# HGRN2 layers: three four-block score visits of 192 columns in place of six two-block visits of 64, with masks kept for one tile

## The reference

```python
q, f, inp_v, g = split(rms_norm(x) @ w_in, 4)      # 1024 columns each
q = silu(q); k = (1 - lb) * sigmoid(-f); log_f = log(lb + (1 - lb) * sigmoid(f))
b = cumsum(log_f)                                   # within a chunk
decay = exp(where(causal, b[t] - b[s], NEG_BIG))
scores = einsum('tk,sk,tsk->ts', q, k, decay)       # decay differs by feature k
o = scores @ v + (q * exp(b)) @ state               # state carried from chunk to chunk
y = rms_norm(o) * o_norm_w * silu(g)
x = x + y @ w_out
```

## Time and profile before

| | before |
|---|---|
| median of 3 runs | 1531.73 us (1531.69 to 1532.85) |
| the profiled execution's own time | 1533.73 us |
| its span in the trace | 1531.9 us |
| TensorE matmul busy | 1455.2 us, 95% of the span |
| VectorE busy | 960.8 us, 63% |
| ScalarE busy | 666.2 us, 43% |
| mean granted TensorE clock | 0.986 of full speed |

### The profile page before, as it was taken

The page is one execution under the profiler, slowest core; times in us unless marked ns, Lnnn a source line. Parts: engine busy times, 40 slices in busy tenths (PEclk is TensorE's granted clock), DMA queues, the critical chain, the costliest instruction groups (busy, mean ns, idle before and its releaser), DMA issues.

```text
span 1531.9 us, 24253 instructions
## 1 busy us (share of the span) xinstructions
PE 1455.2 (95%) x9165; PEld 1301.1 (85%) x9165; DVE 960.8 (63%) x1755; ACT 666.2 (43%) x1174; POOL 6.5 (0%) x16
## 2 busy tenths in 40 slices
PE   7999999989999999999999996699998999999989
PEld 6888888789898989898989895599887988888878
DVE  6677777554566656565666564566656567676772
ACT  5333334233545454545555554344433333433340
POOL 1000000000000000000000000000000000000000
PEclk9999999999999999999999998899999999999999
DMA  6322222233131322222222220043333231322111
GB/s 191 83 61 78 55 66 71 59 100 110 43 97 51 89 56 83 62 78 69 70 70 69 70 70 28 11 120 102 89 99 105 57 83 56 83 56 81 55 55 56
DMA packets 211723, 114.30 MB, mean 75 GB/s; under 512 B 3742, under 2 KB 209744, under 8 KB 211632
## 3 DMA queue, kind: packets, MB, share of 16 engines
q1 hardware_dynamic: 211200, 112.54, 25.6%
q0 software_dynamic: 432, 0.47, 0.1%
HBM read 110.90 MB, written 2.10 MB: 74 GB/s over the span
## 4 chain that ended last, share of the span: by engine, by line
PE 74%; DVE 12%; ACT 8%; issue 5%; DMA 1%; SPq 0%; ACTq 0%; DVEq 0%
PE ps L530 34%; PE ps L542 22%; PE ps L664 5%; ACT scratch L1160 4%; PE ps L810 2%; PE ps L796 2%; PE ps L827 2%; DVE scratch L1682 2%; ACT w_hi L966 2%; DVE scratch L1706 2%; DVE scratch L1690 2%; DVE w_lo L1365 2%; PE ps L693 1%; PE ps L556 1%; PE ps L695 1%
## 5 line engine op out<-in xcount | busy, mean ns | idle before, releaser
L542 PE MATMUL ps<-w_hi,op_hi 128*128 128x256 f32 (+2 forms) x1280 | 418.1, 327 | 17.6 <-DVE op_lo L1409 7.1
L542 PE MATMUL ps<-w_lo,op_hi 128*128 128x256 f32 (+2 forms) x1280 | 404.1, 316 | 0.0
L542 PE MATMUL ps<-w_hi,op_lo 128*128 128x256 f32 (+2 forms) x1280 | 403.9, 316 | 0.0
L530 PE MATMUL ps<-op_hi,w_hi 128*128 128x512 f32 (+1 forms) x800 | 321.5, 402 | 2.2 <-DVE op_lo L1404 2.2
L530 PE MATMUL ps<-op_lo,w_hi 128*128 128x512 f32 (+1 forms) x800 | 307.1, 384 | 0.0
L530 PE MATMUL ps<-op_hi,w_lo 128*128 128x512 f32 (+1 forms) x800 | 306.0, 383 | 0.0
L1365 DVE TENSOR_TENSOR w_lo<-raw,w_hi 128x1024 fp32r<-128x1024 f32 x200 | 242.8, 1226 | 89.8 <-ACT w_hi L966 89.6
L542 PEld LDWEIGHTS ps<-w_hi,op_hi 128*128 128x128 f32 x1280 | 243.9, 191 | 37.3 <-issue 10.1
L542 PEld LDWEIGHTS ps<-w_lo,op_hi 128*128 128x128 f32 x1280 | 243.9, 191 | 5.6
L542 PEld LDWEIGHTS ps<-w_hi,op_lo 128*128 128x128 f32 x1280 | 244.4, 191 | 4.8 <-issue 0.2
L966 ACT ACTIVATE w_hi<-raw 128x1024 fp32r<-128x1024 f32 x200 | 205.1, 1057 | 45.8 <-PE ps L542 30.2
(11 more groups left out here) (174 smaller groups left out, 1571.3 us busy)
## 6 DMA issues: line engine op xcount, KB each, us to landing
raw<-in_b_w_in SPq DMA_DIRECT2D x80, 512.0 KB, 3.7
raw<-in_a_w_in SPq DMA_DIRECT2D x64, 512.0 KB, 4.3
raw<-in_c_w_in SPq DMA_DIRECT2D x24, 512.0 KB, 4.5
raw<-in_a_w_out SPq DMA_DIRECT2D x16, 512.0 KB, 4.3
raw<-in_b_w_out SPq DMA_DIRECT2D x8, 512.0 KB, 4.3
raw<-in_c_w_out SPq DMA_DIRECT2D x8, 512.0 KB, 4.6
xt<-in_x SPq DMA_DIRECT2D x4, 512.0 KB, 8.3
y<-in_norm_w SPq DMA_DIRECT2D x4, 512.0 KB, 4.7
```

Source lines behind the costliest of these rows:

```text
L530: last = nc.tensor.matmul(bank, a, b, start=(k == 0 and p == 0), stop=(k == KT - 1 and p == 2))
L542: last = nc.tensor.matmul(bank, a, b, start=(k == 0 and p == 0), stop=(k == KT - 1 and p == 2))
```

## The change

The six two-block visits with m = 2, 4, ..., 64 become three four-block visits (`quad_scores(r)`) with m = 2, 8, 32. A tile is cut into groups of four blocks of m tokens. The keys are multiplied with three of the four blocks of queries (blocks 1, 2, 3, as they are: 96 columns) and with the same three of a second array `a_far` (96 columns), in which queries have been carried one or two boundaries on: `far_queries` makes blocks 2 and 3, `farthest_queries` makes the one for three blocks back and puts it in the place of block 1. So a visit is four matmuls of 192 columns. Two PSUM banks become one array `scores2`, which each visit fills whole, so every visit waits until the copies of the one before it (`kept`) are done: for visit 0 these are the copies of `scores(0)` and `scores(1)`, `keep_own` and `keep_pairs`. VectorE makes three copies for each visit (384, 256 and 128 elements, `keep_quad(r, 1)` to `keep_quad(r, 3)`), and the masks are stored for one tile and read for all four. The moves stay seven of the queries and seven of the keys. `move_queries(0)` to `farthest_queries(0)` run at the head of the body, `turn_k`, `states` and `values` come one step later, and in body 8 the output splits and the columns of `wide` are placed anew. Cut to its core:

```diff
-G_STEPS = LEVELS + 1
+QUADS = (2, 8, 32)
+G_STEPS = 2 + len(QUADS)
+KEPT = 2 + 3 * len(QUADS)
+QUAD_MASK = 3 * P // 4 + P // 2 + P // 4
+MASKS = P + P // 2 + QUAD_MASK * len(QUADS)
...
                     def scores(g):
-                        q, k, bank = a_q[:, prev], a_k[:, prev], score[g % 2]
-                        if g < 2:
-                            pe.wait_ge(qk_lo_done, h + 1)
-                        else:
-                            pe.wait_ge(upd, h * LEVELS + (g - 1))
-                        if g >= 2:
-                            pe.wait_ge(sd_done, h * 8 + (g - 1))
-                        elif later and g == 0:
-                            pe.wait_ge(st_step, h * 3)
-                        elif later:
-                            pe.wait_ge(sd_done, h * 8)
...
-                            m = 1 << (g - 1)
-                            upper = q.rearrange("p (t b u m) -> p t b u m", t=TT, u=2, m=m)
-                            for t in range(TT):
-                                last = nc.tensor.matmul(bank[:, t * 64:(t + 1) * 64], k[:, t * P:(t + 1) * P],
-                                                        upper[:, t, :, 1, :], start=True, stop=True)
+                        bank = score[g]
+                        pe.wait_ge(qk_lo_done, h + 1)
+                        if later:
+                            if g == 0:
+                                pe.wait_ge(st_step, h * 3)
+                            pe.wait_ge(sd_done, h * KEPT)
+                        cols, to = (slice(0, S), bank[:]) if g == 0 else (slice(S, S + 256), bank[:, 0:256])
+                        nc.tensor.matmul(to, ones_sq, qk_hi[:, cols], start=True, stop=False)
+                        last = nc.tensor.matmul(to, ones_sq, qk_lo[:, cols], start=False, stop=True)
+                        last.then_inc(g_ready, 1)
+
+                    def quad_scores(r):
+
+                        m = QUADS[r]
+                        pe.wait_ge(far_done, h * 6 + 2 * r + 2)
+                        pe.wait_ge(sd_done, h * KEPT + 2 + 3 * r)
+                        for t in range(TT):
+                            tile = slice(t * P, (t + 1) * P)
+                            of = a_qq[:, prev, :, tile].rearrange("p x (h c) -> p x h c", c=4 * m)[:, :, :, m:]
+                            last = nc.tensor.matmul(scores2[:, t * 256:t * 256 + 192], a_k[:, prev, tile], of,
+                                                    start=True, stop=True)
                         last.then_inc(g_ready, 1)
 
...
                     if mix:
                         steps[1] = [turn_v]
-                        for g in range(G_STEPS):
-                            steps.setdefault(int(2 + 2.4 * g), []).append(lambda g=g: scores(g))
-                        steps[21] = [turn_k]
-                        steps[23] = [states]
-                        steps[27] = [values]
+                        for g, at in ((0, 2), (1, 4)):
+                            steps[at] = [lambda g=g: scores(g)]
+                        for r, at in ((0, 5), (1, 11), (2, 17)):
+                            steps[at] = [lambda r=r: quad_scores(r)]
+                        steps[22] = [turn_k]
+                        steps[24] = [states]
+                        steps[28] = [values]
...
                     if mix and not proj:
-                        for k, ks in enumerate((9, 11, 14, 16, 18, 21, 23)):
+                        for k, ks in enumerate((11, 11, 17, 17, 22, 22, 24)):
                             steps[ks].append(lambda k=k: wide(n, k, (0, 1)))
                         for k in range(KT - 3):
-                            steps[27].append(lambda k=k: wide(n, k, (2, 3)))
+                            steps[28].append(lambda k=k: wide(n, k, (2, 3)))
...
+                    def moved(n):
+                        dve.wait_ge(upd, h * LEVELS + n)
+
+                    def kept(count):
+                        dve.wait_ge(sd_done, h * KEPT + count)
+
+                    def far_queries(r):
+
+                        m = QUADS[r]
+                        nb = S // (4 * m)
+                        start = 2 * S - 2 * S // m
+                        decay = a_t[:, prev, start:start + 4 * nb].rearrange("p (b u) -> p b u", u=4)
+                        q = a_q[:, prev].rearrange("p (b u m) -> p b u m", u=4, m=m)
+                        far = a_far[:, prev].rearrange("p (b u m) -> p b u m", u=4, m=m)
+                        moved(2 * r + 1)
+                        nc.vector.tensor_tensor(far[:, :, 2:4], q[:, :, 2:4],
+                                                decay[:, :, 1:3].unsqueeze(3).to_broadcast([P, nb, 2, m]),
+                                                ALU.mult).then_inc(far_done, 1)
+
+                    def farthest_queries(r):
...
+                        dve.wait_ge(far_done, h * 6 + 2 * r + 1)
+                        nc.vector.tensor_tensor(far[:, :, 1], far[:, :, 3],
+                                                decay[:, :, 1].unsqueeze(2).to_broadcast([P, nb, m]),
+                                                ALU.mult).then_inc(far_done, 1)
+
+                    def keep_own():
+                        mask = a_mask[:, 0:P].unsqueeze(1).to_broadcast([P, TT, P])
+                        nc.vector.copy_predicated(a_sd, mask, score[0].rearrange("p (t c) -> p t c", t=TT)).then_inc(sd_done, 1)
+
+                    def keep_pairs():
+                        to = a_sd.rearrange("p t (b u) -> p t b u", u=2)[:, :, :, 1]
+                        mask = a_mask[:, P:P + 64].unsqueeze(1).to_broadcast([P, TT, 64])
+                        nc.vector.copy_predicated(to, mask, score[1][:, 0:256].rearrange("p (t b) -> p t b", t=TT)).then_inc(sd_done, 1)
+
+                    def keep_quad(r, back):
+
+                        m = QUADS[r]
+                        nb = P // (4 * m)
+                        to = a_sd.rearrange("p t (b c) -> p t b c", c=4 * m)[:, :, :, back * m:]
+                        of = scores2[:].rearrange("p (t c) -> p t c", c=256)[:, :, 0:192]
+                        of = of.rearrange("p t (x b c) -> p t x b c", x=2, b=nb)
+                        of = (of[:, :, 0], of[:, :, 1, :, m:], of[:, :, 1, :, 0:m])[back - 1]
+                        at = P + 64 + QUAD_MASK * r + (0, 96, 160)[back - 1]
+                        wide = 4 * m - back * m
+                        mask = a_mask[:, at:at + nb * wide].rearrange("p (b c) -> p b c", b=nb)
+                        nc.vector.copy_predicated(to, mask.unsqueeze(1).to_broadcast([P, TT, nb, wide]),
+                                                  of).then_inc(sd_done, 1)
...
-                    for g in range(8):
+                    if mix:
+                        move_queries(0)
+                        move_keys(0)
+                        far_queries(0)
+                        farthest_queries(0)
+                        if static(h) and h == 0:
+                            dve.wait_ge(s_mask, 16)
+                        if later:
+                            dve.wait_ge(o_ready, h)
+                        taken(0)
+                        gate()
+                        keep_own()
+                    if end:
+                        into_y()
+                    if mix:
+                        taken(1)
+                        kept(1)
+                    if proj:
+                        split_lo_chunk(IN0[n], len(A_PARTS), j, par, 2, a_ring)
+                    elif mix:
+                        split_lo_out(n, 2)
+                    if mix:
+                        keep_pairs()
+                    if proj:
+                        split_lo_chunk(IN0[n], len(A_PARTS), j, par, 3, a_ring)
+                    for r in range(len(QUADS)):
+                        last = r + 1 == len(QUADS)
                         if mix:
-                            taken(g)
-                            gate() if g == 0 else move_on(g)
-                            keep(g)
-                        if mix and not proj and g > 1:
-                            split_y(n, g - 2)
-                        if g == 0 and end:
-                            into_y()
-                        if mix and not proj and g in (1, 2):
-                            split_lo_out(n, g + 1)
-                        if mix and not proj and g in (5, 6, 7):
-                            split_lo_out(n, g - 1)
-                        if proj and g in (1, 2):
-                            split_lo_chunk(IN0[n], len(A_PARTS), j, par, g + 1, a_ring)
-                        if g == 3 and proj:
-                            forget()
-                        if g == 6 and proj:
-                            query()
-                        if g == 7 and proj:
-                            products()
-                        if g >= 4 and proj:
-                            decays({4: (0,), 5: (1, 2), 6: (3, 4), 7: (5, 6)}[g])
-                    if mix and not proj:
-                        split_y(n, 6)
```

(62 more changed lines are left out.)

53 lines of the change are left out of this document (22 added, 31 removed).

## The result

| | before | with the change |
|---|---|---|
| median of 4 runs each | 1532.28 us (1531.69 to 1532.85) | 1549.24 us (1547.27 to 1551.02) |
| the profiled execution's own time | 1533.73 us | 1551.02 us |
| its span | 1531.9 us | 1549.2 us |
| mean granted clock | 0.986 | 0.980 |

The ratio is 1.0108 (1.0092 to 1.0123): 1.1% slower. 1547 was forecast.

What follows compares the result with a forecast made beforehand. TensorE's own list was taken to bound the fourteen bodies with projection and mixing. Per head -1.35 + 1.64 + 0.5 = +0.8, 11.2 in fourteen, plus 4 for body 8: +15, so 1547 us, range 1534 to 1561.

Steps and rivals of the forecast that it cites:

- What the visits save: On TensorE, three visits of 1.31 us replace six of 0.88, saving 1.35 us a head.
- The first wait: TensorE before visit 0 waits for keep_pairs, behind chunk 2's low half on VectorE: 1.64 us a head.
- Visits 1 and 2: VectorE's chain between visits takes 3.7 us against 4.2 of steps, so TensorE has no wait, with 0.5 to spare.
- The second wait: TensorE before the values waits for the end of carry on VectorE: 0.5 us a head.
- The sum of a head: Saving and two waits together: -1.35 + 1.64 + 0.5 = +0.8 us a head, 11.2 in 14 heads.
- Body 8: VectorE's chain sets the time; TensorE waits some 7.5 us, gets back some 2: 2 us a layer, 4 in all.
- The layers between: No separate cost was forecast outside the heads and body 8; the rest was to cost nothing.
- The first wait only: Rival: the values find their states ready, so only the wait before visit 0 costs; 1540 us, chance 0.13.
- VectorE the bound: Rival: copies writing short runs cost the higher rate, so each visit waits, +1 us a head; 1561 us, chance 0.13.
- The visit bound by weight loads: Rival: 192-column records go at the 0.11 us of 64-column ones, a visit 0.9; 1529 us, chance 0.10 with similar ways.
- The falling clock: Rival: the wait in each head drops TensorE to 1.2 GHz, 3.4 us a head; 1595 us, chance 0.03.

Runs made afterwards that it cites:

- e8: e7 with scores(1) one step earlier, turn_o behind step 4 and keep_pairs ahead of into_y on VectorE; 1515.12 us, ratio 0.9886 to the kernel before.
- e1: The changed kernel with keep_pairs, and a memset of one column, ahead of the low half of chunk 2 on VectorE; 1530.40 us, ratio 0.9984.
- e2: The changed kernel with the three visits, turn_k, states and values each one step later; 1541.33 us, ratio 1.0053.
- e7: e4 with the low half of chunk 3 behind the copies of visit 1; 1523.38 us, ratio 0.9932 to the kernel before.
- e3: The changed kernel with only the values one step later, behind step 29; 1544.41 us, ratio 1.0071.
- e9: e8 with body 8 alone changed: output splits ahead of the visits, most wide steps earlier; 1509.84 us, ratio 0.9839 to the kernel before.
- e4: The changed kernel with the edits of e1 and e3 together; 1525.91 us, ratio 0.9952.
- e6: The changed kernel with visits of 96 columns instead of 192, the far queries not multiplied; 1528.16 us, ratio 0.9973.
- e5: The kernel before with masks stored for one tile and read for all four, nothing else; 1533.48 us, ratio 1.0000.

## Why the prediction was right

**What the visits save** was put at 1.35 us a head and is 1.56: 31.61 less 30.05, in e8, where no wait is left in a head. The cost of a new visit, 1.31, was right. The undisturbed step is 0.683 (four from 116.22 to 118.95); visit 1 takes 1.16 and 4.25 with the six steps behind it, so 1.16 + 4.25 - 4.10 = 1.31. The old visit was mis-sized: I took the step as 0.70 from the one behind `scores(1)`, which carries a surplus itself, and so found only 0.07 behind the visit. With 0.683 it is 0.81 + 2.15 - 2.05 = 0.91, and 6 x 0.91 - 3 x 1.31 = 1.53.

**The first wait** was put at 1.64 and is 1.60 + 0.11 = 1.71. The steps to it are there as written: the low half holds VectorE for 1.14, the copy takes 0.72, the signal 0.05, the first visit after a wait 0.11 more. e1 shows its cause and e2 that its length is what counts. e1 gives back only 0.90 of it: its copy still comes 0.25 of shown idle time late, and visit 1 is then late too, which e7 and e8 gave back with 0.30 and 0.52. With the 0.50 of e3 these are 2.22, and the two waits were 1.71 + 0.50 = 2.21.

**Visits 1 and 2** don't wait, as laid. The chain was put at 3.7 from the end of visit 0, signals included, and took 3.9 without the last signal (114.71 to 118.60), so it had 0.35 to spare instead of 0.5.

**The second wait** was put at 0.5; taking it away shortens a head by 0.50. The shown idle time is 3.5 us in fourteen heads, 0.25 each (0.53 at 134.94 is the longest); the overlap of 0.16 and the 0.10 by which the first group after it takes longer (0.71 against 0.61 in the earlier trace rows) make up the rest.

**The sum of a head** was +0.8 and is +0.66, by the larger saving; in fourteen heads 9.2 us instead of 11.2. **Body 8** was put at 4, 2 a layer. From the last q sigmoid of a layer to the square of its last `o_norm` (lines 1114 and 1126 on ScalarE) it takes 3.4 us more than before in layer 0 and 2.6 in layer 3, 6.0 together. TensorE waits there for 7.9 us of shown idle time in both layers, as laid (7.5); what was mis-sized is the 2 us that it should get back, which was 0.6 and 1.4. The clock accounts for the difference between the two layers at most. These are layer 3's visits 0 and 1 and the stretches at a low clock, first of layer 0, then of layer 3:

```profile
1485.35 2.90 PE L674 MATMUL scores<-scratch 128*128 128x192 f32 x8 [4.28 <-DVE scratch L1603]
1491.85 2.92 PE L674 MATMUL scores<-scratch 128*128 128x192 f32 x8 [3.60 <-DVE scratch L1592]
...
273.60:287.20 13.60, 9.27 (x25) 8.00 (x26) 9.55 (x23) 5.31 (x8) 0.00 (x0) 0.51 0.26 77
1483.60:1496.00 12.40, 7.05 (x21) 6.34 (x22) 8.50 (x17) 6.34 (x10) 0.00 (x0) 0.72 0.27 81
```

In layer 0 the clock stands at half for 13.6 us, twice as long as before; in layer 3, behind the same waits, it is at half for some 7 us in all, as before, and that body 8 is 2.6 us longer all the same.

**The layers between,** which the change doesn't touch, were put at nothing and were 1.8 us longer in the profiled execution: 943.3 us against 941.5, from the last `o_norm` of layer 0 to the first q sigmoid of layer 3, with 5943 records of TensorE in both. The clock stood at half for some 41 us of it, against 31 before (added up from stretches of 2 us). In the profiles of all eleven kernels the two go together: 939.9 to 941.5 us in the five with 31 us at half the clock, 941.0 in the one with 34, 941.8 to 943.3 in the five with 41. e8 lies in the first of these groups and e9 in the last, and no run tells what puts an execution into one of them, so this part can't be called an effect of the change.

9.2 + 6.0 + 1.8 are 17.0 of the 17.3 us that the span grew. The mechanism was right in every part; that the total came so near is partly luck, since the heads were put 2.0 too high and the bodies 8 2.0 too low.

**The rivals.** *The first wait only* falls by the fourteen waits for `carry` and by e3. *VectorE the bound* falls by e1 to e4. Its mechanism is half there: in the round with m = 2 the copy of 384 takes 0.73 and with m = 8 0.58, that of 128 0.42 and 0.30; but the slack of that round hid it. The Trainium skill, SBUF — State Buffer, in the section on Door 1, has lines of 16 bytes, full bandwidth with at least two accesses to a line, and a penalty for crossing to a new one. That runs of 2 and of 6 are dearer and runs of 4 (256 elements, 0.43) are not fits the lines; that two accesses to a line are enough is not what the 0.42 for runs of 2 shows. *The visit bound by weight loads* falls by e6. *The falling clock* falls for the heads, where it stayed at 1.00 with a wait of 1.6 us in each; in body 8 it fell, as before the change. The Trainium skill, TensorE: Matmul & The Clock Gate, on oscillation in real kernels, tells of a throttled clock after each wait, in an example with longer waits and less work between them than a head has; the trace agrees in body 8 (waits of 4.28 and 3.60, clock 0.50) and shows none of it in the heads.

## What to carry to other kernels

Where one engine's list is the bound, a change that shortens the list is worth what it saves less every wait that its new order puts in, so lay the rows of both engines side by side from each signal to the first instruction that needs it. The visits with more columns were worth 1.56 us a head here; a wait of 1.71, of which 1.14 was one low half between a signal and a copy, took more than that, and moving the low half made the kernel 0.2% faster than before. Where two buffers become one, each use waits for the last copy of the use before, so the copies go to the front of the other engine's list, and the work that nobody waits for goes behind them.

## What the runs showed of the hardware

- After a wait a visit of eight records takes some 0.11 us longer (1.27 against 1.16; with 96 columns 0.91 against 0.81).
- A mask that is read for all four tiles from one costs the predicated copy nothing (733 ns for 512 elements either way).
- A predicated copy is dearer where it writes short runs, but not only below four elements: 384 elements in runs of 6 took 0.73, in runs of 24 0.58; 128 elements in runs of 2 took 0.42, in runs of 8 0.30.
- The clock is not set by the wait alone. In e5 visit g = 2 of body 8 follows the same wait in both layers, and its clock was full in layer 0 and half in layer 3, whose body 8 took 2.6 us longer:

```profile
267.04 1.11 PE L664 MATMUL ps<-scratch 128*128 128x64 f32 x8 [2.63 <-DVE scratch L1548]
...
1466.88 1.97 PE L664 MATMUL ps<-scratch 128*128 128x64 f32 x8 [2.63 <-DVE scratch L1548]
```

So it was between two kernels: behind a wait of 2.98 us in body 8 of e8 visit 0 took 1.60 us, behind one of 2.99 at the same place in e9 2.90. What tells the cases apart is open. A body 8 or an untouched layer of one profiled execution is therefore no measure of a change below 2 to 3 us.
